# A two-block model step on one core: where the last token tile is turned, and when the last weight slabs are split

## Chip, cores, metric

One NeuronCore of one Trainium2 chip (trn2) runs the whole program. The metric is the time of one execution on the device in microseconds; lower is better. Everything is fp32 in memory.

## The reference

512 tokens of width 1024 go through a first block (three mixers, an MLP) and then through a second block of two layers, which the change is about. In short (`layer_norm`, `rms_norm` and the attentions are as their names say, and `swiglu(h, w_in, w_out)` is `(silu(gate) * up) @ w_out`):

```
for i in range(2):
    h = layer_norm(a * h + 0.5 * swiglu(h, ffa_w_in[i], ffa_w_out[i]), ...)
    proj = h @ mix_w_in[i]      # 1536 q,k,v columns, 512 z, 16 gates, then attention's
    # causal conv of 4, silu, l2 norm of q and k per head (64), gated delta rule, * silu(z)
    # stick-breaking attention, latent attention with rope
    mix = concat(o_gdn, o_sb, o_mla) @ mix_w_o[i]
    h = layer_norm(a * h + mix, ...)
    h = layer_norm(a * h + 0.5 * swiglu(h, ffb_w_in[i], ffb_w_out[i]), ...)
    h = h + sigmoid(h @ ple_w_gate[i]) * (p[i] @ ple_w_proj[i])
```

The feed-forward has 2816 inner columns. The result is `h`, 512 x 1024.

## The kernel before

**Operands.** Each projection is computed from operands split in two fp32r parts: `hi` is the rounded value, `lo` the rest. `mm3` (L243) makes three matmuls of one product: hi x hi, hi x lo, lo x hi. Weights come in slabs of 2048 fp32 a partition through a ring of three slots. SyncE loads a slab into `K.raw[z]`, ScalarE rounds it into `K.hi[z]`, VectorE subtracts into `K.lo[z]`; slab `j` uses slot `j % 3`. `ahead` (L442 for VectorE, L459 for ScalarE) is called as an engine walks over the slabs in program order, and splits up to one slab ahead of the one that TensorE is at. ScalarE's rounding waits until TensorE has used the slab that was in that slot (`w used`), and SyncE's load until that slab was split. `K.fences` (`stop`) hold the splitting back where the ring's memory is lent to another stage.

**Order.** Each engine's program is a list written by hand, stage by stage (`tensor_program`, `vector_program` and so on), and each engine works strictly in that order. Engines wait for each other by named points (`K.at`). PSUM banks are taken in rotation (`take`).

**Two shapes of projection.** `pe_fm` keeps a weight block stationary and streams all 512 tokens, so it needs all four token tiles of 128. `pe_tm` keeps a token tile stationary and streams up to 512 weight columns; a slab then holds 4 row blocks of 128.

**Closings.** The MLP, each feed-forward and each mixer output end with `pe_by_tile`: the last 512 of 1024 columns, whose two slabs are both taken at the start, tile by tile, 24 matmuls each. When a tile is complete, VectorE adds it to `hX` and applies the norm (`dve_ln`, or `dve_final` after the MLP). TensorE then transposes it (8 transposes, `pe_tiles`), and ScalarE and VectorE split the transposed tile into `hL` (`act_tiles`, `dve_tiles`), the operand of the next projection. `tiles_after` says that tile i-1 is transposed behind tile i, and tile 3 right behind tile 2 at the end. `pe_ple` closes layer 0 in the same way, without a norm. The walk `tm_walk` of ScalarE and VectorE calls `ahead` for a group of slabs and then handles its four tiles, so the second slab of a closing is split by VectorE behind the four tiles of the first 512 columns.

**Mixer input** (`pe_mx_in`, L2524). 12 blocks of 128 columns by `pe_fm`. Behind block f, `job(f - 1)` sums the squares of a q or k block on TensorE or transposes a v block. Then come the 16 gate columns by `pe_tm`, with 16-column matmuls on four tiles; then eight fp32 matmuls spread the reciprocal norms over the partitions (`mx rn`); then the 512 `z` columns. VectorE scales q and k by the spread norms (`dve_mx_scale`), computes the gates, and the delta rule begins.

**Attention** lends itself the ring's `hi` and `lo` memory (`lender`). The `raw` slots keep loading, but nothing is split until the stage is over (fence `ring back 4`). Behind it `act_split` and `dve_split` split the 8 blocks of `catT`, and only then the first slab of the mixer output.

## Time and profile before

| | us |
|---|---|
| runs, median of 3 (lowest, highest) | 4786.41 (4783.46, 4788.29) |
| profiled execution, whole time | 4790.0 |
| its span, first to last instruction | 4788.2 |
| TensorE busy (share of the span) | 4233.6 (88%) |
| VectorE, ScalarE, GpSimd busy | 2180.8, 1340.5, 156.6 |
| mean granted TensorE clock | 0.914 |

A row of the profile names the engine (PE is TensorE, PEld its weight loads, DVE VectorE, ACT ScalarE, POOL GpSimd, SP SyncE), the line of the kernel, the operation, output<-input and the shapes. Since helpers record all operations, L232 is every matmul, L239 every transpose, L286 every `tensor_tensor`, L297 every `scalar_tensor_tensor` and L336 every activation. `ring` is the lent or raw part of the weights' memory, `r` a rounded operand (`hi`, `lo`, `hL`), and `arena` the rest. A matmul `128*128 128x512` has 128 rows by 128 stationary columns and streams 512. Clock 1.00 is 2.4 GHz and 0.50 is 1.2 GHz.

### The profile page before, as it was taken

To read this page: it belongs to the slowest core of one execution; us is meant where nothing else is said; L and a number is where in the kernel's file an instruction comes from. 1 tells how busy PE (TensorE), PEld (TensorE's weight loads), DVE (VectorE), ACT (ScalarE), POOL (GpSimd) and SP (SyncE) were. 2 spreads that over 40 slices of the span, in tenths; PEclk is the share of its full clock that TensorE was granted. 3 is DMA by queue.
4 is the path that set the end of the run, shared out by engine and by line. 5 is a ranking of instruction groups with operands and counts; after the bars stand their busy time and mean duration, and the time that the engine had idled before them with its cause. 6 is when DMAs were issued, how large, how long until landed. Compare 5 with 4: busy or idle time off the path is not lost.

```text
span 4788.2 us, 69852 instructions
## 1 busy us (share of the span) xinstructions
PE 4233.6 (88%) x30212; PEld 3338.8 (70%) x30212; DVE 2180.8 (46%) x2940; ACT 1340.5 (28%) x1886; POOL 156.6 (3%) x194
## 2 busy tenths in 40 slices
PE   6987878878677999999987989998999987989998
PEld 3855768856455787788666667887788666567886
DVE  2135467753744444433636344334333636444334
ACT  3133233312122232322221342222222321342222
POOL 0000012120000000000001000000000001000000
PEclk8878979989889999999978989999999978999999
DMA  5101000033123323233200113232333200112331
GB/s 191 45 1 44 9 2 3 3 110 105 53 71 109 117 96 105 80 93 93 71 28 16 40 39 89 85 106 86 95 94 91 63 19 15 40 53 80 97 100 54
DMA packets 319059, 322.10 MB, mean 67 GB/s; under 512 B 10032, under 2 KB 243552, under 8 KB 317984
## 3 DMA queue, kind: packets, MB, share of 16 engines
q1 hardware_dynamic: 312144, 287.53, 19.5%
q0 software_dynamic: 6608, 30.11, 1.7%
q8 instruction: 238, 3.90, 0.3%
q14 instruction: 69, 0.57, 0.0%
...
## 4 chain that ended last, share of the span: by engine, by line
PE 77%; DVE 13%; issue 4%; ACT 4%; DMA 1%; POOL 0%; DVEq 0%; ACTq 0%; POOLq 0%
PE psum L232 76%; DVE ring L286 3%; DVE arena L297 3%; DVE ring L317 2%; DVE arena L286 2%; PE psum L239 1%; ACT arena L336 1%; ACT ring L336 1%; ACT r L336 1%; DVE r L286 1%; DVE arena L293 1%; DMA ring<-in_rw_g 0%; DVE arena L317 0%; DVE arena L291 0%; DVE ring L301 0%
## 5 line engine op out<-in xcount | busy, mean ns | idle before, releaser
L232 PE MATMUL psum<-r 128*128 128x512 f32 (+3 forms) x12912 | 3024.5, 396 | 157.0 <-DVE r L286 141.3
L232 PEld LDWEIGHTS psum<-r 128*128 128x128 f32 (+1 forms) x12912 | 2429.3, 195 | 748.6 <-DVE r L286 90.7
L286 DVE TENSOR_TENSOR r<-ring,r 128x2048 fp32r<-128x2048 f32 (+2 forms) x269 | 580.2, 2157 | 411.6 <-ACT r L336 400.6
L336 ACT ACTIVATE arena<-psum 128x512 f32<-128x512 f32 (+4 forms) x456 | 249.2, 547 | 1306.9 <-PE psum L232 1211.5
L336 ACT ACTIVATE r<-ring 128x2048 fp32r<-128x2048 f32 (+2 forms) x269 | 484.3, 1800 | 417.7 <-PE psum L232 341.1
L232 PE MATMUL psum<-arena 64*64 64x64 f32 (+14 forms) x2384 | 403.9, 337 | 48.7 <-DVE arena L286 17.8
L232 PE MATMUL psum<-ring 64*64 64x64 f32 (+4 forms) x8608 | 352.3, 236 | 84.2 <-ACT ring L336 34.8
L232 PEld LDWEIGHTS psum<-arena 128*128 128x128 f32 (+6 forms) x2384 | 265.2, 187 | 177.4 <-issue 131.7
L232 PEld LDWEIGHTS psum<-ring 64*64 64x64 f32 (+3 forms) x8608 | 290.6, 145 | 125.6 <-issue 47.5
L286 DVE TENSOR_TENSOR arena<-arena,psum 128x512 f32<-128x512 f32 (+2 forms) x192 | 114.9, 598 | 577.2 <-PE psum L232 570.2
L232 PE MATMUL psum<-ring,arena 64*64 64x64 f32 (+6 forms) x2464 | 265.4, 292 | 100.0 <-DVE ring L286 34.5
L297 DVE SCALAR_TENSOR_TENSOR arena<-arena 128x512 f32<-128x512 f32 (+4 forms) x316 | 266.7, 844 | 118.5 <-ACT arena L336 107.4
L232 PEld LDWEIGHTS psum<-ring,arena 64*64 64x64 f32 (+4 forms) x2464 | 148.8, 156 | 185.7 <-issue 136.9
L336 ACT ACTIVATE ring<-psum 128x512 f32<-128x512 f32 (+5 forms) x276 | 148.7, 539 | 457.6 <-PE psum L232 342.6
L336 ACT ACTIVATE r<-arena 128x512 fp32r<-128x512 f32 (+1 forms) x176 | 109.4, 622 | 530.4 <-DVE arena L286 528.4
L232 PE MATMUL psum<-arena,ring 64*64 64x64 f32 (+6 forms) x3072 | 203.7, 257 | 31.5 <-DVE ring L286 21.6
L286 DVE TENSOR_TENSOR arena<-arena 128x512 f32<-128x512 f32 (+7 forms) x273 | 171.1, 628 | 127.3 <-ACT arena L336 117.0
L286 DVE TENSOR_TENSOR arena<-psum,arena 128x512 f32<-128x512 f32 (+4 forms) x112 | 71.2, 636 | 343.9 <-PE psum L232 267.5
L232 PEld LDWEIGHTS psum<-arena,ring 64*64 64x64 f32 (+4 forms) x3072 | 166.7, 162 | 61.8 <-DVE ring L286 28.9
L286 DVE TENSOR_TENSOR r<-arena,r 128x512 fp32r<-128x512 f32 (+1 forms) x176 | 119.7, 680 | 157.4 <-ACT r L336 154.4
L336 ACT ACTIVATE arena<-arena 128x512 f32<-128x512 f32 (+10 forms) x181 | 78.1, 432 | 373.0 <-DVE arena L293 205.6
L239 PE MATMUL psum<-arena 128*128 128x128 f32 (+2 forms) x612 | 95.0, 307 | 98.7 <-DVE arena L291 48.0
...
## 6 DMA issues: line engine op xcount, KB each, us to landing
...
```

Of the source, the lines that this page charges most:

```text
L232: ins = self.raw.matmul(o, l, r, start=start, stop=stop, skip_group_check=True)
L239: ins = self.raw.transpose(o, i, self.K.C["ident"])
L286: self.done(self.raw and self.raw.tensor_tensor(o, a, b, f), keys)
L293: self.done(self.raw and self.raw.tensor_scalar(o, a, s1, s2, f0, f1), keys)
L297: self.done(self.raw and self.raw.scalar_tensor_tensor(out=o, in0=a, scalar=s, in1=b, op0=f0, op1=f1), keys)
L317: self.done(self.raw and self.raw.copy_predicated(o, m, d), keys)
L336: self.done(self.raw and self.raw.activation(o, i, f, scale=scale, bias=bias), keys)
```

## The change

- **Tiles.** `pe_tiles` transposes only tile i-1. Tile 3 is transposed inside the next projection. At a feed-forward's first slab and at the mixer input's first two blocks, `pe_halves` runs both blocks on tokens 0 to 255, then transposes tile 3 (`pe_tile`), then runs both on tokens 256 to 511. At the gated embedding, `pe_tm` waits by tile and transposes tile 3 ahead of its last tile. ScalarE and VectorE keep their order: they split tile 3 as the last step of the closing stage.
- **Slabs.** `tm_walk(both=True)` calls `ahead_of` once more before the four tiles of the first 512 columns in a closing stage.
- **Gate columns.** The 16 gate columns' weights become stationary with 512 tokens streamed, ahead of `job(11)`. ScalarE copies the 16 x 512 result, and four small matmuls turn it. The matmuls for the norms (`to_all`) move into `z`'s first slab, before its last tile, in the four banks that `z` does not hold.
- **Attention.** Each slot's `hi` and `lo` lie side by side; attention is lent those of slots 0 and 1 only, and the slab that follows it is put into slot 2 (`add_slab`, `next_slot`) and may be split before attention. `m.sq` and `m.st` move to scratch. Waits on `j - NSLOT` become waits on the last slab in the same slot.
- **`pT`** is loaded before the norm's rows on GpSimd's queue, without waiting for the end of the feed-forward.

```diff
+    def add_slab(self, pieces, size, split):
+        z = self.next_slot
+        self.slabs.append((pieces, size, split))
+        self.slot.append(z)
+        self.same_slot.append(self.last_in.get(z))
+        self.last_in[z], self.next_slot = len(self.slabs) - 1, (z + 1) % NSLOT
...
-            z, (_, size, split) = j % NSLOT, K.slabs[j]
+            z, (_, size, split) = K.slot[j], K.slabs[j]
-                if j >= NSLOT:
-                    a.wait_ge(*K.at("w used", j - NSLOT))
+                if K.same_slot[j] is not None:
+                    a.wait_ge(*K.at("w used", K.same_slot[j]))
...
+                if within and (done, k0, i) == (0, 0, len(tiles) - 1):
+                    within()
+                    if by_tile:
+                        t.wait_ge(*K.at(by_tile, "lo", i, q // 4))
...
-def tm_walk(E, ncols, kt, tiles, step=512):
+def tm_walk(E, ncols, kt, tiles, step=512, both=False):
+        if both and done == 0:
+            E.ahead_of()
...
+def pe_tile(t, K, st, x, ready):
+    t.wait_ge(*K.at(*ready, x))
+    for half in range(2):
+        o = t.take(st, "tr", x, half)
+        for q in range(4):
+            f = 4 * half + q
+            t.tr(o[:, 128 * q:128 * q + 128], K.m.hX[:, x, 128 * f:128 * f + 128],
+                 *([(st, "tr", x, half)] if q == 3 else []))
-    for x in tiles_after(i):
-        t.wait_ge(*K.at(*ready(x)))
-        for half in range(2):
-            o = t.take(st, "tr", x, half)
-            for q in range(4):
-                f = 4 * half + q
-                t.tr(o[:, 128 * q:128 * q + 128], K.m.hX[:, x, 128 * f:128 * f + 128],
-                     *([(st, "tr", x, half)] if q == 3 else []))
+    if i:
+        pe_tile(t, K, st, i - 1, ready)
+def pe_halves(t, K, wh, wl, blocks, st, ready):
+    for half in range(2):
+        c = slice(256 * half, 256 * half + 256)
+        for o, js, keys in blocks:
+            for k in range(8):
+                t.wait_ge(*K.at(st, "lo", 2 * half + 1, k // 4))
+                t.mm3(o[:, c], wh[:, k, js], wl[:, k, js], K.m.hL[:, 0, k, c], K.m.hL[:, 1, k, c],
+                      half == 0 and k == 0, half == 1 and k == 7, *(keys if half == 1 and k == 7 else []))
+        if half == 0:
+            pe_tile(t, K, st, 3, ready)
...
-                 *[(st, "lo", 4 * half + q) for q in range(4)])
+                 (st, "lo", x, half))
...
-def lender(K, first=SLOT * NSLOT):
+def lender(K, first=SLOT * NSLOT, end=RING):
-        assert used[0] <= RING, used[0]
+        assert used[0] <= end, used[0]
...
-    K.hi = [parts[:, SLOT * z:SLOT * z + SLOT] for z in range(NSLOT)]
-    K.lo = [parts[:, SLOT * (NSLOT + z):SLOT * (NSLOT + z) + SLOT] for z in range(NSLOT)]
+    K.hi = [parts[:, 2 * SLOT * z:2 * SLOT * z + SLOT] for z in range(NSLOT)]
+    K.lo = [parts[:, 2 * SLOT * z + SLOT:2 * SLOT * z + 2 * SLOT] for z in range(NSLOT)]
...
-    lend = lender(K)
+    lend = lender(K, end=RING - 2 * SLOT)
...
-    m.st = lend(128)
-    m.sq = lend(512)
+    m.sq, m.st = m.tmp[:, 0:512], m.tmp[:, 512:640]
+    m.pop = A.operand(2, 512)
+    m.sgp = view(al(2048), [512, 4], [1, 512])
+    A.top = base + 10240
-    m.pop = A.operand(2, 512)
-    K.base = base
-    m.sgp = view(al(2048), [512, 4], [1, 512])
...
             wh, wl = view(wh, [256, 8], [1, 256]), view(wl, [256, 8], [1, 256])
+            if part == 0 and f == 0:
+                blocks = [(t.take("ff1", l, j, 0, 0, u), slice(128 * u, 128 * u + 128),
+                           [("ff1", l, j, 0, 0, u)] + ([("w used", i)] if u else [])) for u in range(2)]
+                pe_halves(t, K, wh, wl, blocks, ready, source)
+                continue
             for u in range(2):
                 for k in range(8):
-                    t.wait_ge(*K.at(ready, "lo", k))
                     t.mm3(o, wh[:, k, js], wl[:, k, js], m.hL[:, 0, k, :], m.hL[:, 1, k, :], k == 0, k == 7,
     pe_by_tile(t, K, ("ff2", l, j, 2), Wo, 128 * FF_PARTS[2][0], 512, 512, FF_PARTS[2][1], m.hop, ("ff h", l, j, 2), 512,
-               lambda i: pe_tiles(t, K, st, i, lambda x: ("ln x", l, j, x)))
+               lambda i: pe_tiles(t, K, st, i, ("ln x", l, j)))
...
-    pe_fm(t, K, ("mx u", l), K.I["mix_w_in_2"][l], 0, 1536, 8, m.hL, lambda f: SEGS[0:1], ready=("hT", l, 0),
-          among=others, after=lambda f, g: job(f - 1))
+    W = K.I["mix_w_in_2"][l]
+    i, wh, wl = t.chunk(W, 0, 8, 0, 256)
+    blocks = [(t.take(("mx u", l), f, 0, among=others), slice(128 * f, 128 * f + 128),
+               [(("mx u", l), f, 0)] + ([("w used", i)] if f else [])) for f in range(2)]
+    pe_halves(t, K, wh, wl, blocks, ("hT", l, 0), ("ln x", l, 0))
+    job(0)
+    pe_fm(t, K, ("mx u", l), W, 0, 1536, 8, m.hL, lambda f: SEGS[0:1], among=others, after=lambda f, g: job(f - 1), start=256)
+    i, wh, wl = t.chunk(W, 0, 8, 2048, 16)
+    o = t.take("mx ab", l, among=others)
+    for k in range(8):
+        t.mm3(o[0:16, :], wh[:, k, :], wl[:, k, :], m.hL[:, 0, k, :], m.hL[:, 1, k, :], k == 0, k == 7,
+              *([("mx ab", l), ("w used", i)] if k == 7 else []))
-    pe_tm(t, K, ("mx ab", l), K.I["mix_w_in_2"][l], 2048, 16, 8, m.hL, W512)
-    for f in range(8):
-        o = t.take("mx rn", l, f)
-        t.wait_ge(*K.at("mx rn", l))
-        t.mm(o, m.hb[0:16, 128 * f:128 * f + 128], m.rn[0:16], True, True, ("mx rn b", l, f))
-    pe_tm(t, K, ("mx z", l), K.I["mix_w_in_2"][l], 1536, 512, 8, m.hL, W512)
+    def to_all():
+        z = [K.bank_of[("mx z", l), 0, i][0] for i in range(4)]
+        for f in range(8):
+            o = t.take("mx rn", l, f, among=tuple(b for b in BANKS if b not in z))
+            t.wait_ge(*K.at("mx rn", l))
+            t.mm(o, m.hb[0:16, 128 * f:128 * f + 128], m.rn[0:16], True, True, ("mx rn b", l, f))
+    o = t.take("mx ab T", l)
+    t.wait_ge(*K.at("mx ab sb", l))
+    for i in range(4):
+        t.mm(o[:, 16 * i:16 * i + 16], m.abT[0:16, 128 * i:128 * i + 128], C["ident"][0:16, 0:16], True, True,
+             *([("mx ab T", l)] if i == 3 else []))
+    pe_tm(t, K, ("mx z", l), W, 1536, 512, 8, m.hL, W512, within=to_all)
...
+    E.ahead()
+    a.wait_ge(*K.at("mx ab", l))
+    a.copy(m.abT[0:16], K.bank("mx ab", l)[0:16, :], ("mx ab sb", l))
+    K.free(a, "mx ab", l)
-    for _ in tm_walk(E, 16, 8, 4):
-        pass
...
+    E.ahead()
-    for c, i, _ in tm_walk(E, 16, 8, 4):
-        v.wait_ge(*K.at(("mx ab", l), c, i))
-        v.copy(m.gab[:, i, :], K.bank(("mx ab", l), c, i)[:, 0:16], ("mx gab", l))
-        K.free(v, ("mx ab", l), c, i)
+    v.wait_ge(*K.at("mx ab T", l))
+    v.copy(view(m.gab, [1, 64]), K.bank("mx ab T", l)[:, 0:64], ("mx gab", l))
+    K.free(v, "mx ab T", l)
...
     dve_split(v, K, ("cat", l), m.catT, m.hL, 8)
-    for c, i, _ in tm_walk(E, 1024, 8, 4):
+    for c, i, _ in tm_walk(E, 1024, 8, 4, both=True):
         x = m.hX[:, i, c:c + 512]
...
-    g.wait_ge(*K.at(("ff2", l, 2, 2), 512, 3))
-        pe_tm(t, K, ("ple g", l, hf), K.I["ple_w_gate_2"][l], 512 * hf, 512, 8, m.hL, W512, ready=("hT", l, "p"))
+        pe_tm(t, K, ("ple g", l, hf), K.I["ple_w_gate_2"][l], 512 * hf, 512, 8, m.hL, W512, by_tile=("hT", l, "p"),
+              within=None if hf else (lambda: pe_tile(t, K, ("hT", l, "p"), 3, ("ln x", l, 2))))
-                   lambda i: pe_tiles(t, K, ("hT", 0, 2), i, lambda x: ("ple x", 0, 1, x)) if (l, hf) == (0, 1) else None)
+                   lambda i: pe_tiles(t, K, ("hT", 0, 2), i, ("ple x", 0, 1)) if (l, hf) == (0, 1) else None)
...
         E.meet(f"attention {l}, ring lent")
+        if K.counting:
+            K.next_slot = NSLOT - 1
         pe_attention(E, K, l)
         E.meet(f"ring back 4 {l}")
-        K.fences[E.slab] = f"ring back 4 {l}"
+        K.fences[E.slab + 1] = f"ring back 4 {l}"
         pe_mix_out(E, K, l)
-        pe_ff(E, K, l, 2, "ffb_w_in_2", "ffb_w_out_2", ("hT", l, 1), ("hT", l, "p"))
+        pe_ff(E, K, l, 2, "ffb_w_in_2", "ffb_w_out_2", ("hT", l, 1), ("ln x", l, 1), ("hT", l, "p"))
         pe_ple(E, K, l)
...
         E.wait_ge(*K.at("ln x", l, 1, 3))
+        pool_ple(E, K, l)
         pool_ln(E, K, l, 2)
-        pool_ple(E, K, l)
         E.wait_ge(*K.at("ln x", l, 2, 3))
```

## Rows read from the trace of the kernel before

**Rows 1.** Page: busy time by engine; chain that ended last, by engine.
```profile
PE 4233.6 (88%) x30212; PEld 3338.8 (70%) x30212; DVE 2180.8 (46%) x2940; ACT 1340.5 (28%) x1886; POOL 156.6 (3%) x194
...
PE 77%; DVE 13%; issue 4%; ACT 4%; DMA 1%; POOL 0%; DVEq 0%; ACTq 0%; POOLq 0%
```

**Rows 2.** Waits of TensorE: total us, times, longest.
```profile
PE psum L232 <- DVE r L286: 141.3, 28, 17.9
...
PE psum L239 <- DVE arena L297: 27.6, 7, 4.0
```

**Rows 3.** Chain of waits, closing of layer 0's second feed-forward: start, us, what.
```profile
3271.15 0.87 PE psum L239 x8
3272.02 5.62 PE psum L232 x24
...
3284.16 0.70 DVE arena L297
...
3289.03 0.70 DVE r L286
...
3291.46 3.75 PE psum L232 x8
```

**Rows 4.** Groups by form, 549 to 557.6 us (busy us, mean ns).
```profile
L232 PE MATMUL psum<-r 128*128 128x256 f32 x24 | 3.1, 285 | 0.0
```

**Rows 5.** Timeline of the same closing: start, us, engine, what, [idle before].
```profile
3253.42 1.91 ACT L336 ACTIVATE r<-ring 128x2048 fp32r<-128x2048 f32 x1 [9.32 <-PE psum L232]
...
3254.70 4.67 DVE L286 TENSOR_TENSOR r<-ring,r 128x2048 fp32r<-128x2048 f32 x2
```

**Rows 6.** Timeline of TensorE, first slabs of the first and last closing.
```profile
1907.11 13.02 PE L232 MATMUL psum<-r 128*128 128x512 f32 x48 [3.76 <-DVE r L286]
...
4683.81 14.06 PE L232 MATMUL psum<-r 128*128 128x512 f32 x48 [3.75 <-DVE r L286]
```

**Rows 7.** Stretches: us, busy us per engine, then clock (PEclk), DMA share, GB/s.
```profile
2294.10:2308.30 14.20, 14.20 (x50) 11.19 (x51) 6.75 (x8) 0.20 (x1) 0.00 (x0) 0.78 0.47 148
...
2413.00:2433.60 20.60, 20.60 (x98) 20.60 (x97) 5.91 (x5) 7.71 (x7) 0.00 (x0) 0.50 0.17 52
2433.60:2447.60 14.00, 14.00 (x18) 5.19 (x17) 7.09 (x9) 0.00 (x0) 0.00 (x0) 0.50 0.23 75
...
549.00:557.60 8.60, 8.60 (x51) 7.46 (x50) 4.87 (x5) 2.92 (x5) 0.00 (x0) 1.00 0.00 1
...
3303.00:3340.00 37.00, 37.00 (x161) 29.76 (x160) 11.14 (x11) 8.38 (x9) 0.00 (x0) 1.00 0.32 85
```

**Rows 8.** Timeline, next projection behind the MLP and at layer 0's mixer input.
```profile
1940.22 81.15 PE L232 MATMUL psum<-r 128*128 128x512 f32 x337 [1.10 <-DVE r L286]
...
2328.65 12.49 PE L232 MATMUL psum<-r 128*128 128x512 f32 x48
```

**Rows 9.** Timeline of VectorE at that mixer input.
```profile
2329.46 0.92 DVE L321 MEMSET arena<- 128x1032 f32 x1 [0.16 <-issue]
...
2336.72 2.33 DVE L297 SCALAR_TENSOR_TENSOR arena<-arena 128x512 f32<-128x512 f32 x3
...
2339.75 0.69 DVE L286 TENSOR_TENSOR arena<-arena 128x512 f32<-128x512 f32 x1 [0.70 <-ACT arena L336]
```

**Rows 10.** Timeline at layer 0's gate columns.
```profile
2412.55 0.86 PE L239 MATMUL psum<-arena 128*128 128x128 f32 x4 [4.86 <-ACT arena L336]
...
2416.08 3.34 DVE L309 RECIPROCAL arena<-arena 16x512 f32<-16x512 f32 x1 [3.53 <-ACT arena L336]
```

**Rows 11.** Groups by form, 96 stationary columns.
```profile
L232 PE MATMUL psum<-r 128*96 128x512 f32 x96 | 22.7, 395 | 0.0
```

**Rows 12.** Timeline between attention and mixer output, layer 0.
```profile
2832.75 6.26 DVE L286 TENSOR_TENSOR r<-arena,r 128x512 fp32r<-128x512 f32 x8 [2.96 <-ACT r L336]
...
2841.64 20.59 PE L232 MATMUL psum<-r 128*128 128x512 f32 x78 [10.70 <-DVE r L286]
```

**Rows 13.** Timeline of VectorE before attention.
```profile
2695.33 0.69 DVE L286 TENSOR_TENSOR arena<-psum,arena 32x512 f32<-32x512 f32 x1 [17.87 <-PE psum L232]
```

More of the change, by code:

```diff
@@ L113, in __init__ @@
         self.signals, self.points, self.meets, self.slabs, self.fences, self.late = {}, {}, {}, [], {}, {}
+        self.slot, self.same_slot, self.last_in, self.next_slot = [], [], {}, 0
         self.counting = True
@@ L268, in weights @@
         if K.counting:
-            K.slabs.append((pieces, size, split))
-        z = i % NSLOT
+            K.add_slab(pieces, size, split)
+        z = K.slot[i]
         if split:
@@ L373, in load, with pe_fm @@
         K.points[("in", *key)] = (K.load_sem[z], K.loads[z])
-def pe_fm(t, K, st, W, c0, ncols, kt, xs, segs, ready=None, among=BANKS, after=None):
-    for done in range(0, ncols, 256):
+def pe_fm(t, K, st, W, c0, ncols, kt, xs, segs, ready=None, among=BANKS, after=None, start=0):
+    for done in range(start, ncols, 256):
         n = min(256, ncols - done)
@@ L397, in pe_fm, with pe_tm @@
                     after((done + m) // 128, g)
-def pe_tm(t, K, st, W, c0, ncols, kt, xs, tiles, r0=0, ready=None, step=512, among=BANKS):
+def pe_tm(t, K, st, W, c0, ncols, kt, xs, tiles, r0=0, ready=None, step=512, among=BANKS, by_tile=None, within=None):
     for done in range(0, ncols, step):
@@ L467, in ahead_of @@
             j = self.n_split
-            z, (_, size, split) = j % NSLOT, K.slabs[j]
+            z, (_, size, split) = K.slot[j], K.slabs[j]
             if split:
                 a.wait_ge(*K.at("w in", j))
-                if j >= NSLOT:
-                    a.wait_ge(*K.at("w used", j - NSLOT))
+                if K.same_slot[j] is not None:
+                    a.wait_ge(*K.at("w used", K.same_slot[j]))
                 a.copy(K.hi[z][:, 0:size], K.raw[z][:, 0:size], ("w hi", j))
@@ L480, in sync_program @@
     for j, (pieces, size, split) in enumerate(K.slabs):
-        z = j % NSLOT
+        z, b = K.slot[j], K.same_slot[j]
         if j in K.late:
             e.after(K.late[j])
-        if j >= NSLOT:
-            if K.slabs[j - NSLOT][2]:
-                e.wait_ge(*K.at("w hi", j - NSLOT))
-                e.wait_ge(*K.at("w lo", j - NSLOT))
+        if b is not None:
+            if K.slabs[b][2]:
+                e.wait_ge(*K.at("w hi", b))
+                e.wait_ge(*K.at("w lo", b))
             else:
-                e.wait_ge(*K.at("w used", j - NSLOT))
+                e.wait_ge(*K.at("w used", b))
         for fn, src in pieces:
@@ L871, in memory @@
     m.cv = view(al(1024), [512, 2], [1, 512])
-    m.rn = al(512)
+    m.rn, m.abT = al(512), al(512)
     m.hb = view(m.ktok, [1, 1024])
@@ L2288, in pe_mlp @@
     pe_by_tile(t, K, ("mlp2", 3), K.I["w_mlp2"], 3072, 512, 512, 8, m.hop1, ("mlp h", 3), 512,
[L2289 removed]
+               lambda i: pe_tiles(t, K, ("hT", -1, 2), i, ("fin x",)))
 def act_mlp(E, K):
@@ L2306, in act_mlp @@
             a.copy(m.hop1[:, 0, f, :], m.tmp1[:, 1024 + 512 * (f % 2):1536 + 512 * (f % 2)], (("mlp h", part), "hi", f))
-        for c, i, _ in tm_walk(E, 1024, 8, 4):
+        for c, i, _ in tm_walk(E, 1024, 8, 4, both=part == 3):
             if part == 3 and c:
@@ L2322, in dve_mlp @@
             v.tt(m.hop1[:, 1, f, :], o2, m.hop1[:, 0, f, :], SUB, (("mlp h", part), "lo", f))
-        for c, i, _ in tm_walk(E, 1024, 8, 4):
+        for c, i, _ in tm_walk(E, 1024, 8, 4, both=part == 3):
             o = m.tmp1[:, 512 * (i % 2):512 * (i % 2) + 512]
@@ L2430, with pe_ff @@
 FF_PARTS = ((0, 8), (8, 6), (14, 8))
-def pe_ff(E, K, l, j, wi, wo, ready, st):
+def pe_ff(E, K, l, j, wi, wo, ready, source, st):
     t, m = TensorLine(E, "ff"), K.m
@@ L2475, in act_ff @@
             a.copy(m.hop[:, 0, f, :], m.tmpf[:, 1024 + 512 * z:1536 + 512 * z], (("ff h", l, j, part), "hi", f))
-        for c, i, _ in tm_walk(E, 1024, nt, 4):
+        for c, i, _ in tm_walk(E, 1024, nt, 4, both=part == 2):
             if part == 0:
@@ L2503, in dve_ff @@
             v.tt(m.hop[:, 1, f, :], o2, m.hop[:, 0, f, :], SUB, (("ff h", l, j, part), "lo", f))
-        for c, i, _ in tm_walk(E, 1024, nt, 4):
+        for c, i, _ in tm_walk(E, 1024, nt, 4, both=part == 2):
             x = m.hX[:, i, c:c + 512]
@@ L3347, in act_mix_out @@
     act_split(a, K, ("cat", l), K.m.catT, K.m.hL, 8)
-    for c, i, _ in tm_walk(E, 1024, 8, 4):
+    for c, i, _ in tm_walk(E, 1024, 8, 4, both=True):
         if c:
@@ L3356, in dve_mix_out @@
     dve_split(v, K, ("cat", l), m.catT, m.hL, 8)
-    for c, i, _ in tm_walk(E, 1024, 8, 4):
+    for c, i, _ in tm_walk(E, 1024, 8, 4, both=True):
         x = m.hX[:, i, c:c + 512]
@@ L3526, in vector_program @@
         E.meet(f"attention {l}, ring lent")
+        E.ahead_of()
         dve_attention(E, K, l)
@@ L3578, in scalar_program @@
         E.meet(f"attention {l}, ring lent")
+        E.ahead_of()
         act_attention(E, K, l)
```

5 lines of the change are left out of this document (2 added, 3 removed).

## The prediction

> **What bounds the kernel now.** I read the page first: TensorE is busy 88% of the span and 77% of the chain that ended last, VectorE holds 13% of that chain, ScalarE 4% and DMA 1% [rows 1]. The reader is to see that TensorE sets the time and that what can be won lies in its idle stretches, which VectorE ends most often. The list of TensorE's waits names the two kinds that the change aims at: 28 waits for a VectorE write of an `r` tile (141.3 us) and 7 waits of 3.98 us for the layer norm [rows 2]. Then I read the timeline where one projection closes and the next begins, and last the granted clock by stretches.
>
> Unit prices: in an undisturbed closing, 24 matmuls of 512 columns take 5.62 us and 8 transposes 0.87 us in the chain [rows 3]. That is 0.234 us a matmul and 11.24 us for the 48 that use one full slab. At 256 columns 24 of them take 3.1 us at clock 1.00, 0.129 each [rows 4].
>
> **A. Both last slabs split together.** Seven projections close by tiles: the MLP, four feed-forwards, two mixer outputs. Each needs two slabs at its first tile, and the second one's `lo` is made on VectorE only after its two steps on the last tile of the columns before. TensorE stands 3.75 to 3.79 us; 7 times, 26.3 us. The 48 matmuls behind the gap are slow: 13.02, 14.26, 12.99, 14.07, 13.94, 12.98 and 14.06 us against 11.24 (the first and the last are shown [rows 6]), together 16.6 us. The clock of the second one is 0.78 [rows 7], so it runs partly at 1.2 GHz instead of 2.4, behind the idle time. After the change the slot of that slab is free when TensorE leaves the first slab of the earlier columns, 11.24 us before the gap's place. ScalarE's rounding (1.91) and VectorE's subtraction (2.3) need 4.2 [rows 5], so 7 us of cover is left. VectorE's first tile queues behind that split for about 1.5 us, and nobody waits for it, since tiles come 2.8 us apart. Gain 42.9; ends 26.3 (the slow clock stays) and 43.
>
> **B. The last tile turned inside the next projection.** From the last matmul of a closing to the next projection's first, the path is VectorE's norm (about 4.8 us from 3284.16), 0.87 of transposes and three 0.70 steps of splitting [rows 3]. The eight places cost 7.3, 7.35, 7.6, 7.5, 4.7, 7.5, 7.6 and 7.5 us (MLP, feed-forward, mixer output, feed-forward, gated embedding of layer 0, and the last three kinds again in layer 1), 57.0 in all [rows 3, 8]. After: 0.87 for tile 2, then a half projection (48 half-width matmuls, 6.2 us) that outlasts the 4.8 us of the norm, then 0.87 for tile 3. Then comes a wait for its first half: ScalarE 0.64, VectorE 0.70 and hand-overs, less the 0.44 that the second half's transposes cover, 1.1. Then the other half. The half width costs 96 x 0.129 - 48 x 0.234 = 1.15 us.
> - Four feed-forward starts: 2 x 0.87 + 1.1 + 1.15 = 4.0 each, 16. The second slab's split now queues behind tile 3 on both engines and is ready about 5.1 us after its transposes, while TensorE needs it after 7.3: no wait.
> - Two gated embeddings (full width, tile 3 turned after three tiles): 2 x 0.87 + 1.1, and there the second slab comes 1.2 late, since only 12 matmuls (2.8 us) stand between: 4.0 each, 8.
> - Two mixer inputs: 4.0, plus a new wait. Behind tile 3 VectorE has the clearing of `ubg` (0.92) and the split (2.29) before it convolves block 0 (0.5 + 2.33), then wait for ScalarE's SiLU (0.70) and square it (0.69) [rows 9]. That ends 11.0 us after the transposes, and both blocks end at 7.3: 3.7 us at the first sum of squares. 7.7 each, 15.4.
>
> Sum 39.4, gain 17.6. The clock cost here too: at the feed-forward after the MLP 337 matmuls took 81.15 instead of 79.0, and at the mixer input 48 took 12.49 instead of 11.24 [rows 8]; over the eight places some 16.6 us. The new stalls are shorter but not gone, so I count half, 8. Gain 25.6. Ends: nothing (no clock back and 2.2 us more queueing at each place) and 34.2.
>
> By the Trainium skill, page "TensorE: Matmul & The Clock Gate", section "Back-to-back issue gap", matmuls of 256 and 512 columns cost 262 and 518 cycles, so halving the width would cost next to nothing and the sum would gain about 6 us more. The trace disagrees: 0.129 against half of 0.234. The page "Perfetto Trace Analysis", section "Matmuls", says that larger matmuls are more efficient. That rule speaks against this edit, and the trace agrees, with 1.15 us a place.
>
> **C. Gate columns and norms.** In layer 0 from the last block (2407.1) to the end of `z` (2471.3) lie 64.2 us: a 4.86 wait for ScalarE's SiLU, 96 matmuls of 16 columns in 20.6, eight fp32 products of 512 columns in 14.0, `z` in 24; both middle stretches ran at clock 0.50 [rows 7, 10]. In layer 1 it is 65.8. After: 24 matmuls of 512 columns with 16 columns stationary (as 96 columns stationary, 22.7 us for 96 [rows 11]) take 5.65 and cover the wait for the SiLU. The last turns take 0.9, to 2413.3. Then `z`'s first slab is late: ScalarE rounds it after the SiLU (to 2414.4) and VectorE subtracts to 2416.7. Copying the gate rows and the four small products fit in that. `z` takes 22.5. The reciprocal of the norms (3.34 [rows 10]), now behind that split and ScalarE's root with its table load, ends near 2422.7, and TensorE asks for it at 2425.1. The eight products then cost 0.86 each at full clock (half of 14.0): 6.9. VectorE's scaling of 0.69 a block keeps pace, so four banks do. End 2446.1, plus 1.7 for a clock that falls behind the 3.4 us stall: 40.7. Gain 23.5, and 25.1 in layer 1: 48.6. Ends: 23 (clock at half throughout: 5.6 more for the gate columns, 7.1 for the products, in both layers) and 52.
>
> **D. Attention lends two slots.** Between attention and the mixer output TensorE stands 10.70 us: ScalarE and VectorE first split the eight blocks of `catT` (6.26 on VectorE), then the first slab [rows 12]. With the first slab split in the idle time before attention (VectorE stands 17.87 us there [rows 13]), the first matmul needs only block 0, at 2833.5: 8.1 earlier, less 0.3 because the first tile is paced by VectorE's 0.78 a block. VectorE is through with `catT` at 2839.0 and with the second slab 2.3 later; TensorE needs that at 2845. Gain 7.8 a layer, 15.6. The first 78 matmuls took 20.59 instead of 18.3 [rows 12]. I leave these 2.3 us as they are, since the clock may be low from attention's thin work; they are the upper end. Ends 10 and 20. The earlier load of `pT`, the moved scratch and the slot order count nothing: the loads are hidden by 5 us landings on a queue that is mostly idle; without that cover a late load would cost its 4 to 5 us.
>
> **Sum.** 42.9 + 25.6 + 48.6 + 15.6 = 132.7. The profiled execution took 4790.0 (span 4788.2 and 1.8 around it), so 4657; the median of the runs, 4786.4, lies 3.6 lower, so 4654. I forecast 4655. All good ends give 149, all bad ones 59.
>
> **Rivals.**
> 1. The clock does not come back. If the falls follow from changes in activity and not from these gaps, A keeps 26.3, B 17.6, C 23, D 15.6: 83, so 4704. For it: the gate columns ran at 0.50 although TensorE was busy all through [rows 7]. Against: the 37 us from 3303 have clock 1.00 with no gap in them [rows 7]. Chance 0.14.
> 2. The in-order queues take the place of the norm. ScalarE and VectorE now stand at tile 3 until its transposes come, so splits and first activations slip; with 5 us more at each of the eight places 40 us go: 4694. For it: the mixer input, where I already find 3.7. Against: VectorE is busy 46% of the span [rows 1]. Chance 0.17.
> 3. Slower: half clock that holds. The gate columns show TensorE fully busy and at 0.50 for 34.6 us [rows 7]. If half-width matmuls with a stall between them hold it so at all eight places, each loses 17.3 us, 138 in all, against 132.7 - 8 gained: 4786 + 13, 4800. It decides from about 31 us a place. Against: half-width matmuls ran at 1.00 from 549 on [rows 4, 7]. Chance 0.05.
> 4. The edits don't do what they say (the slab still comes last, the rows for the norms late): within 0.2%, chance 0.03.
>
> The page "TensorE: Matmul & The Clock Gate", section "HAM oscillation — how this bites in real kernels", says that idle gaps between bursts throttle the array each time. By that rule all the clock of A and B returns and the sum would be 8 us larger. The rows behind the gaps agree with it; the fully busy gate columns at 0.50 it does not explain by idle time alone.
>
> **How the numbers follow.** Main case 0.61, by itself 4635 to 4680. With rivals 1 and 2 the range is 4632 to 4706. What a measurement of this kernel can tell from no change is 0.2%, 9.6 us. Faster: 0.61 + 0.14 + 0.17 = 0.92; same 0.03; slower 0.05.
>
> **What would show it.** A is right if no 3.75 us gap stands before the 48 matmuls of a closing and they take 11.2 to 11.5 us. B is right if the time from the last full-width matmul of a closing to the end of the next slab's work falls from 18.6 to about 15.2, with one wait near 1.1 us; at the mixer input a wait near 3.7 us stands before the first sum. C: the stage from the last block to the end of `z` takes about 41 us and its clock is 1.00 for the most part; if it reads 0.50, rival 1 gains. D: 2 to 3 us instead of 10.70. A clock below 1.00 for tens of us behind the half-width matmuls would show rival 3 and make the prediction wrong.

## The result, and the profile after

The changed kernel takes 4665.2 us (median of four runs, 4662.8 to 4673.4), the kernel before 4784.9 (4783.2 to 4788.3): 0.9752 of the time, 95% interval 0.9735 to 0.9769. The forecast was 4655, in a range of 4632 to 4706. The profiled execution took 4664.5 (span 4662.7), 125.5 us less than that of before; the forecast said 132.7. By the medians the gain is 119.7.

In the rows of this kernel and of the experiments L241 is every matmul, L248 every transpose, L295 every `tensor_tensor`, L306 every `scalar_tensor_tensor` and L345 every activation. The list of TensorE's waits shows what went (total us, times, longest): the `r` waits of 141.3 us [rows 2] are 106.7, and the seven waits for the norm (27.6 us) are gone from the list's first ten.

```profile
PE psum L241 <- DVE r L295: 106.7, 26, 17.9
PE psum L241 <- DVE ring L295: 66.0, 30, 9.4
PE psum L241 <- ACT ring L345: 48.4, 27, 5.4
```

**The places of the change**, TensorE's timeline of after (start, length, what, [idle before <- who ended it]). First the closing behind layer 0's second feed-forward and the gated embedding, against [rows 3, 6]:

```profile
3194.66 18.20 PE L241 MATMUL psum<-r 128*128 128x512 f32 x77
...
3213.49 5.87 PE L241 MATMUL psum<-r 128*128 128x512 f32 x24
...
3226.47 8.65 PE L241 MATMUL psum<-r 128*128 128x512 f32 x36
3234.95 1.04 PE L248 MATMUL psum<-arena 128*128 128x128 f32 x8
3236.97 3.06 PE L241 MATMUL psum<-r 128*128 128x512 f32 x12 [0.98 <-DVE r L295]
3241.06 5.16 PE L241 MATMUL psum<-r 128*128 128x512 f32 x21 [1.03 <-DVE r L295]
```

The 3.75 us gap has gone, tile 3's transposes stand within the projection, and two short waits remain: 0.98 for its split (forecast 1.1) and 1.03 for the second slab (forecast 1.2). Next the place behind the MLP, where the forecast saw no further wait:

```profile
1923.45 5.86 PE L241 MATMUL psum<-r 128*128 128x256 f32 x48
1929.15 1.03 PE L248 MATMUL psum<-arena 128*128 128x128 f32 x8
1931.16 17.11 PE L241 MATMUL psum<-r 128*128 128x256 f32 x96 [0.98 <-DVE r L295]
1952.74 42.56 PE L241 MATMUL psum<-r 128*128 128x512 f32 x172 [4.48 <-DVE r L295]
```

The half-width start is there (the 96 are 48 of half and 48 of full width), and a new wait of 4.48 us ahead of the third slab. Layer 0's mixer input, gates and `z`, against [rows 7, 8, 10]:

```profile
2313.79 5.87 PE L241 MATMUL psum<-r 128*128 128x256 f32 x48 [0.98 <-DVE r L295]
2324.09 1.89 PE L241 MATMUL psum<-arena 128*16 128x512 f32 x2 [4.43 <-DVE arena L295]
2325.91 7.51 PE L241 MATMUL psum<-r 128*128 128x512 f32 x24
...
2392.98 5.77 PE L241 MATMUL psum<-r 128*16 128x512 f32 x24
2398.59 0.60 PE L248 MATMUL psum<-arena 128*128 128x128 f32 x4
2402.81 1.88 PE L241 MATMUL psum<-arena 16*128 16x16 f32 x8 [3.63 <-DVE arena L300]
2404.63 10.21 PE L241 MATMUL psum<-r 128*128 128x512 f32 x36
2414.77 10.54 PE L241 MATMUL psum<-arena 16*128 16x512 f32 x16
2425.25 15.75 PE L241 MATMUL psum<-r 128*128 128x512 f32 x60
```

The gate columns cost 5.77 us (forecast 5.65). But `z`'s first 36 matmuls take 10.21 instead of 8.4, the norm products 10.54 instead of 6.9, and the last 60 15.75 instead of 14.0. The windows of the same stretches (granted clock in the third column from the end) say why, and that TensorE was busy all the time:

```profile
2402.80:2414.70 11.90, 11.89 (x44) 9.65 (x44) 5.76 (x3) 3.91 (x4) 0.00 (x0) 0.78 0.55 178
2414.80:2425.20 10.40, 10.40 (x17) 3.83 (x16) 4.81 (x7) 0.00 (x0) 0.00 (x0) 0.67 0.00 0
2425.30:2440.80 15.50, 15.50 (x61) 12.46 (x61) 1.72 (x7) 6.56 (x10) 0.00 (x0) 0.90 0.00 0
```

At the mixer output the first matmul waits 2.65 us instead of 10.70 [rows 12]:

```profile
2801.54 36.51 PE L241 MATMUL psum<-r 128*128 128x512 f32 x144 [2.65 <-DVE r L295]
```

**Where the time went, by stages.** The profiled executions are cut at instructions that all kernels share, on VectorE unless said: "fin" is the last tile's reciprocal behind the MLP; "first" and "close" are the first statistics of a norm and its fifth (the closing's tile 0); "set" clears `ubg`; "z end" is the first small gate product on TensorE. The columns e1 to e12 are the experiments of the next section. Us from one mark to the next (five rows of layer 1 that repeat those of layer 0 within 1 us are left out):

```
to                  before  after   e1     e2     e3     e4     e10    e5     e6     e7     e8     e9     e11    e12
fin                 1936.2 1925.9 1925.7 1919.0 1928.4 1926.3 1922.5 1927.5 1928.5 1925.3 1925.2 1924.3 1922.9 1928.8
ffa0 first           346.5  348.2  347.3  347.3  348.1  348.1  348.1  348.8  341.2  348.1  348.1  348.2  341.3  341.2
ffa0 close            20.8   12.7   20.4   12.7   12.7   12.7   12.7   12.7   12.7   12.7   12.7   12.7   12.7   12.7
mx0 set               26.0   28.0   28.0   26.0   28.0   28.0   28.0   28.0   28.0   28.0   27.9   28.0   28.0   28.0
z0 end               141.9  126.1  125.9  124.8  143.6  126.1  126.1  125.0  126.3  122.3  122.1  115.4  111.6  114.8
mo0 first            387.4  379.8  383.2  380.4  386.8  383.9  395.1  383.7  383.9  383.4  381.1  387.1  380.6  387.8
mo0 close             19.6   12.6   19.6   12.6   12.6   12.6   12.6   12.6   12.6   12.6   12.6   12.6   12.6   12.6
ffb0 first           367.3  362.1  360.8  368.5  362.1  362.1  362.1  362.1  362.1  362.1  362.1  362.1  362.1  362.1
ffb0 close            20.6   12.7   20.8   12.7   12.7   12.7   12.7   12.7   12.7   12.7   12.7   12.7   12.7   12.7
ffa1 first           437.0  430.4  427.9  438.3  429.4  429.4  429.3  430.4  429.4  430.4  429.4  430.3  430.4  430.4
z1 end (from set)    143.3  125.6  124.4  124.8  142.2  124.3  126.5  124.1  124.4  122.6  119.4  113.5  110.4  114.8
mo1 first            392.4  381.3  385.0  383.5  382.2  386.2  390.8  382.8  382.9  381.0  381.7  379.9  386.3  388.8
end (from ffb1 cl.)   95.2   89.4   89.4   94.9   89.4   89.4   89.4   89.4   89.4   89.4   89.4   89.4   89.4   89.4
```

Two kinds of stage are to be told apart. Those of full matmuls repeat to 0.1 us from kernel to kernel where the code is the same ("ffa1 first", with the embedding in it, to 1.1). "fin" and "mo first" hold much thin work, and where the code up to them is the same ("fin": all but before and e1; "mo first": all but before, e10 and e12) they vary from 1919.0 to 1928.8 and from 379.8 to 387.1. So a median can't show an edit worth under 5 us; its stage can.

### The profile page after: what moved, and what is told of

It is laid out like the page before. It is cut to its first block, busy times and chain, and to the rows that moved or that the text cites. A ratio compares the mean times of both kernels' runs of the same rounds, so it can differ in the third digit from the quotient of the medians.

```text
span 4662.7 us, 70153 instructions
## 1 busy us (share of the span) xinstructions
PE 4166.8 (89%) x30372; PEld 3297.4 (71%) x30372; DVE 2180.1 (47%) x2934; ACT 1340.6 (29%) x1888; POOL 157.7 (3%) x194
## 4 chain that ended last, share of the span: by engine, by line
PE 69%; issue 12%; DVE 12%; ACT 4%; DMA 1%; POOL 0%; DVEq 0%; ACTq 0%; SPq 0%; POOLq 0%
PE psum L241 68%; DVE ring L295 2%; DVE arena L306 2%; DVE ring L326 2%; DVE arena L295 2%; PE psum L248 1%; ACT arena L345 1%; ACT r L345 1%; ACT ring L345 1%; DVE r L295 1%; DVE arena L302 1%; DMA ring<-in_w_ada 0%; DVE arena L300 0%; DMA ring<-in_rw_g 0%; DVE arena L326 0%
## 5 line engine op out<-in xcount | busy, mean ns | idle before, releaser
L241 PE MATMUL psum<-r 128*128 128x512 f32 (+3 forms) x13056 | 2977.3, 389 | 122.4 <-DVE r L295 106.7
L241 PEld LDWEIGHTS psum<-r 128*128 128x128 f32 x13056 | 2392.2, 191 | 701.8 <-DVE r L295 79.1
L295 DVE TENSOR_TENSOR r<-ring,r 128x2048 fp32r<-128x2048 f32 (+2 forms) x269 | 580.4, 2158 | 452.4 <-ACT r L345 442.5
L345 ACT ACTIVATE arena<-psum 128x512 f32<-128x512 f32 (+3 forms) x458 | 250.3, 546 | 1249.7 <-PE psum L241 1158.0
L345 ACT ACTIVATE r<-ring 128x2048 fp32r<-128x2048 f32 (+2 forms) x269 | 484.5, 1801 | 406.1 <-PE psum L241 330.2
L241 PE MATMUL psum<-arena 64*64 64x64 f32 (+15 forms) x2400 | 399.6, 334 | 62.9 <-DVE arena L295 26.6
L241 PE MATMUL psum<-ring 64*64 64x64 f32 (+4 forms) x8608 | 351.0, 235 | 84.7 <-ACT ring L345 34.3
L241 PEld LDWEIGHTS psum<-arena 128*128 128x128 f32 (+7 forms) x2400 | 264.8, 186 | 187.8 <-issue 125.3
L241 PEld LDWEIGHTS psum<-ring 64*64 64x64 f32 (+3 forms) x8608 | 289.2, 144 | 124.5 <-issue 46.2
L295 DVE TENSOR_TENSOR arena<-arena,psum 128x512 f32<-128x512 f32 (+2 forms) x192 | 114.8, 598 | 552.6 <-PE psum L241 545.6
L241 PE MATMUL psum<-ring,arena 64*64 64x64 f32 (+6 forms) x2464 | 258.4, 289 | 100.2 <-DVE ring L295 33.0
L306 DVE SCALAR_TENSOR_TENSOR arena<-arena 128x512 f32<-128x512 f32 (+4 forms) x316 | 266.7, 844 | 119.0 <-ACT arena L345 107.7
L345 ACT ACTIVATE ring<-psum 128x512 f32<-128x512 f32 (+5 forms) x276 | 148.7, 539 | 451.2 <-PE psum L241 374.2
L241 PEld LDWEIGHTS psum<-ring,arena 64*64 64x64 f32 (+4 forms) x2464 | 147.1, 156 | 181.9 <-issue 132.2
L345 ACT ACTIVATE r<-arena 128x512 fp32r<-128x512 f32 (+1 forms) x176 | 109.4, 622 | 518.8 <-DVE arena L295 516.8
L295 DVE TENSOR_TENSOR arena<-arena 128x512 f32<-128x512 f32 (+8 forms) x289 | 176.8, 613 | 127.9 <-ACT arena L345 117.0
L241 PE MATMUL psum<-arena,ring 64*64 64x64 f32 (+6 forms) x3072 | 201.7, 255 | 32.6 <-DVE ring L295 21.9
L241 PEld LDWEIGHTS psum<-arena,ring 64*64 64x64 f32 (+4 forms) x3072 | 166.4, 161 | 61.2 <-DVE ring L295 30.1
L295 DVE TENSOR_TENSOR arena<-psum,arena 128x512 f32<-128x512 f32 (+4 forms) x112 | 71.2, 636 | 292.6 <-PE psum L241 235.0
L295 DVE TENSOR_TENSOR r<-arena,r 128x512 fp32r<-128x512 f32 (+1 forms) x176 | 119.8, 681 | 157.3 <-ACT r L345 154.4
L345 ACT ACTIVATE arena<-arena 128x512 f32<-128x512 f32 (+10 forms) x181 | 78.1, 432 | 323.1 <-DVE arena L302 168.1
L326 DVE COPY_PREDICATED ring<-arena,psum 128x512 f32<-128x512 uint32 (+1 forms) x202 | 136.0, 679 | 37.5 <-PE psum L241 30.9
```

Of the source, the lines that this page charges most:

```text
L241: ins = self.raw.matmul(o, l, r, start=start, stop=stop, skip_group_check=True)
L295: self.done(self.raw and self.raw.tensor_tensor(o, a, b, f), keys)
L306: self.done(self.raw and self.raw.scalar_tensor_tensor(out=o, in0=a, scalar=s, in1=b, op0=f0, op1=f1), keys)
L326: self.done(self.raw and self.raw.copy_predicated(o, m, d), keys)
L345: self.done(self.raw and self.raw.activation(o, i, f, scale=scale, bias=bias), keys)
```

## The experiments

**Each part undone alone.** In e1 the three walks lose `both`. e2 turns tile 3 behind tile 2 and starts at full width:

```diff
 def pe_tiles(t, K, st, i, ready):
     if i:
         pe_tile(t, K, st, i - 1, ready)
+    if i == 3:
+        pe_tile(t, K, st, 3, ready)
```

e3 puts back the old `act_mx_in` and `dve_mx_in`, the 16-column matmuls, and the products ahead of `z`. e4 drops the two added calls `E.ahead_of()` ahead of attention, and e10 the shifted fence too:

```diff
-            K.fences[E.slab + 1] = f"ring back 4 {l}"
+            K.fences[E.slab] = f"ring back 4 {l}"
```

e1: 

> Part A undone alone: the second of the two last slabs is split at the first tile of the last columns again, seven closings. Theory (gap and slow clock belong together): between the traces of before and after, the aligned points give 5.0 to 6.8 us a closing, 42 in all, so this kernel takes 4665 + 42 = 4707 us; a gap near 3.8 us stands before each closing and the 48 matmuls behind it take 13 to 14 us. Rival (the clock recovered for other reasons): only the gaps of 3.75 us come back, 26 us, 4691, and the 48 matmuls stay at 11.2 to 11.5.

e2: 

> Part B undone alone: tile 3 is turned right behind tile 2 and every projection behind it starts at full width, once all of its input is split; the gated embedding too. Theory (the eight places gave 23 us by the aligned points: 6 to 8 each behind feed-forwards, 5 to 8 at the embedding, but -0.3 at the feed-forward behind the MLP and -2.3 and -1.3 at the two mixer inputs): 4665 + 23 = 4688, and the stage from layer 0's feed-forward to the end of block 11 of the mixer input gets about 2 us shorter than in the kernel after. Rival (what the aligned points show at these places is the clock's own coming and going, and only the shorter waits count): 4665 + 9 = 4674.

e3: 

> Part C undone alone: 96 matmuls of 16 moving columns for the gates, the eight norm products before z. Theory: the stage from the turn behind block 11 to the end of z goes back to 64 to 66 us in both layers, +33 us, 4698. Rival (the part is worth what was forecast and the rest was lost elsewhere by the change of phase): +48.6, 4714.

e4: 

> Part D undone in its effect: the two slots are still lent and loaded early, but ScalarE and VectorE split the first slab of the mixer output after the eight blocks of catT. Theory: the split in the idle time before attention is all of the gain, the gap of 10.7 us comes back in both layers, +16 us, 4681. Rival (part of the gain is the earlier load): less than +12 us, a gap under 8 us.

e10: 

> Part D undone for good: the fence stands before the mixer output's first slab again and no slab is split before attention, so it is loaded and split behind the eight blocks of catT. Theory (the place of the split is the gain; in e4 the ordinary look-ahead had already made it, so the explicit call changed nothing): the gap of 2.65 us becomes 10.7 in both layers, +16 us, 4681. Rival (e4's reading: the part is worth 3 us): 4668.

Measured: e1 4707.6 us, e2 4689.7, e3 4704.6, e4 4668.1, e10 4685.1 (0.9833, 0.9799, 0.9828, 0.9753 and 0.9789 of before, intervals of plus or minus 0.0015). Against 4665.2 the parts are worth 42.4, 24.5, 39.5 and, by e10, 19.9, 126 in all, where the whole change gives 119.7. The intervals are 7 us to either side, so each of these differences is known to some 10 us only, and the stages say more. e1's closing has the gap and the slow matmuls behind it again, where after has neither, as the first theory says (4707 expected):

```profile
2284.42 13.83 PE L241 MATMUL psum<-r 128*128 128x512 f32 x48 [3.75 <-DVE r L295]
```

e2's timeline at the mixer output has the wait for the norm and the transposes at half speed behind it; its stages say 6.4 and 6.3 us at the second feed-forwards, 7.9 over the first embedding and the feed-forward behind it, 5.5 at the last embedding, but -0.9 behind the MLP and -3.3 and -2.7 at the mixer inputs (both stages to "z end" added):

```profile
2845.36 1.97 PE L248 MATMUL psum<-arena 128*128 128x128 f32 x8 [3.98 <-DVE arena L306]
2847.98 4.25 PE L241 MATMUL psum<-r 128*128 128x512 f32 x10 [0.65 <-DVE r L295]
```

e3's stages give C 17.5 and 16.6, 34.1 in all, as its theory says (33); the median lies between theory and rival. e4's theory fell: its wait at the mixer output is 2.65 us as in after, since with the fence one slab later the ordinary look-ahead splits that slab anyway (VectorE's split stands at 2658.23, ahead of attention, as in after at 2654.23), and the added calls do nothing. e10 undoes what matters, and the old wait is back, in both layers:

```profile
2814.66 35.18 PE L241 MATMUL psum<-r 128*128 128x512 f32 x144 [10.70 <-DVE r L295]
```

**The price of half width (e5).**

```diff
-                for k in range(8):
-                    t.mm3(o, wh[:, k, js], wl[:, k, js], m.hL[:, 0, k, :], m.hL[:, 1, k, :], ...
+                for c in (slice(0, 256), slice(256, 512)):
+                    for k in range(8):
+                        t.mm3(o[:, c], wh[:, k, js], wl[:, k, js], m.hL[:, 0, k, c], m.hL[:, 1, k, c], ...
```

> The disputed unit price by itself: all 84 remaining feed-forward blocks run as 96 matmuls of 256 columns instead of 48 of 512, with nothing else changed. Theory (the trace after shows 48 of them in 5.70 us, 0.119 each, so the width costs 0.2 us a block): +10 to +20 us, 4675 to 4685. Rival (0.129 each, as the prediction read it: 1.15 us a block): +97 us, 4762.

4674.5 us by the median, 9 more than after, but hardly any of it in the changed stages: "ffb0 first", with 21 slabs halved, is 362.1 us in both, and all four feed-forwards together are 1.4 us longer for 84 slabs. Half width costs next to nothing, and the rival's 97 us are refuted. The 277 matmuls of the timeline stand 32.48 / 277 = 0.117 us apart, half of 0.234:

```profile
2867.78 32.48 PE L241 MATMUL psum<-r 128*128 128x256 f32 x277
```

**Three orders (e6, e7, e8).** e6 moves the rotary tables from block 0 to block 4 in both queues. e7 moves one call, e8 two:

```diff
-    job(0)
-    pe_fm(..., after=lambda f, g: job(f - 1), start=256)
+    pe_fm(..., after=lambda f, g: (f == 2 and job(0), job(f - 1)), start=256)
```

```diff
 def act_mx_in(E, K, l):
...
         K.free(a, ("mx u", l), f, 0)
+        if f == 11:
+            E.ahead()
         a.wait_ge(*K.at("mx conv", l, f))
...
-    E.ahead()
     a.wait_ge(*K.at("mx ab", l))
 def dve_mx_in(E, K, l):
...
-    E.ahead()
     v.wait_ge(*K.at("mx sums", l, 7))
...
     K.free(v, "mx sums", l)
+    E.ahead()
```

e6: 

> The rotary tables (about ten small VectorE steps and two sines on ScalarE) are made at block 4 of layer 0's first feed-forward instead of block 0. Theory (they stood in both queues ahead of the split of the third slab, which the half start needs 6 us sooner after tile 3's turn, and made the new 4.48 us wait): the wait goes, the clock behind it holds, -4.5 to -7 us, 4659 to 4661. Rival (the splits of tile 3 and of the slab are late by themselves): the wait stays above 3 us, no change.

e7: 

> At the mixer input the first sum of squares is issued behind block 2 instead of before it. Theory (TensorE waits 4.43 us there for block 0's square, which nobody needs before block 2's square): the wait goes in both layers, -8.9 us and up to 2 us of clock each, 4652 to 4656. Rival (the wait only moves: block 2's weights or the convolution of block 1 are late next): -2 us or less.

e8: 

> Gates: VectorE makes the sum for the norms before it splits z's first slab (it frees the bank that the turned gate rows take), and ScalarE rounds that slab before the last SiLU. Theory (the 3.63 us stall is this order, and the low clock of the norm products comes from the stall): the stall falls under 1 us and the sixteen passes of the norm products take 7 us instead of 10.5, so -3 - 3.5 - up to 2 for z, in both layers: -13 to -17 us, 4648 to 4652. Rival (the fp32 products on 16 rows lower the clock themselves): the stall goes but the products stay at 9 to 10.5 us, -6 us, 4659.

Measured: 4665.5, 4665.7 and 4654.8 us. By the medians e6 and e7 are worth nothing, by their stages 7.0 us (348.2 to 341.2) and 3.8 and 3.0; e11 below shows these gains in a median too. In e6 no wait stands behind the first 0.97, so the first theory holds:

```profile
1933.75 61.63 PE L241 MATMUL psum<-r 128*128 128x256 f32 x287 [0.97 <-DVE r L295]
```

e7 is between its two theories: of 4.43 us of waiting, 0.28 + 1.67 + 0.72 remain, because VectorE convolves and splits without a pause there:

```profile
2319.32 5.86 PE L241 MATMUL psum<-r 128*128 128x512 f32 x24 [0.28 <-DVE r L295]
2325.11 1.03 PE L241 MATMUL psum<-arena 128*16 128x512 f32 x2
2327.81 1.03 PE L241 MATMUL psum<-arena 128*16 128x512 f32 x2 [1.67 <-DVE arena L295]
...
2335.36 1.03 PE L241 MATMUL psum<-arena 128*16 128x512 f32 x2 [0.72 <-DVE arena L295]
```

e8 settles the cause of C's loss, timeline and windows of the same stretches:

```profile
2398.70 1.03 PE L241 MATMUL psum<-arena 16*128 16x16 f32 x8 [0.33 <-ACT arena L345]
2399.67 8.66 PE L241 MATMUL psum<-r 128*128 128x512 f32 x36
2408.26 11.65 PE L241 MATMUL psum<-arena 16*128 16x512 f32 x16
```

```profile
2399.70:2408.20 8.50, 8.50 (x37) 6.65 (x36) 5.77 (x3) 4.83 (x5) 0.00 (x0) 1.00 0.41 125
2408.30:2419.80 11.50, 11.50 (x17) 4.12 (x16) 4.82 (x7) 0.00 (x0) 0.00 (x0) 0.60 0.27 90
2419.90:2435.90 16.00, 16.00 (x61) 12.81 (x61) 1.72 (x7) 6.56 (x10) 0.00 (x0) 0.86 0.00 0
```

The stall is 0.33 instead of 3.63 us and `z` starts at full clock, but the norm products fall to 0.60 with TensorE busy before and during them. The rival was right: they lower the clock themselves. In layer 0 the 112 matmuls of `z` and products take as long as in after (8.66 + 11.65 + 16.29 = 36.6 us against 36.5), so without the stall the same clock is lost later, and what is gained is the stall and the faster gate products in front of it. In layer 1 they take 34.9 instead of 37.6. The stage gains 4.0 and 6.2.

**The products in rounded passes (e9).**

```diff
-            t.mm(o, m.hb[0:16, ...], m.rn[0:16], True, True, ("mx rn b", l, f))
+            t.mm(o, m.hb[0:16, ...], m.rr[0:16, 0], True, False)
+            t.mm(o, m.hb[0:16, ...], m.rr[0:16, 1], False, True, ("mx rn b", l, f))
```

`rr` holds the norms in two rounded parts, made by one copy on ScalarE and one subtraction on VectorE.

> The order of e8, and the eight norm products as two passes of rounded operands (the norms split in two by ScalarE and VectorE, the zeros and ones exact) instead of fp32 passes: again sixteen matmuls of 512 columns on 16 rows. Theory (fp32 passes on 16 rows lower the clock, 0.58 with TensorE busy all through in e8, and the rounded ones don't): sixteen at 0.234 would take 3.8 us, held up by VectorE's scaling to 5 to 6, and the 60 matmuls of z behind take 14.1 us instead of 16.3 and 16.8: about 8 us a layer less than e8, 4639. Rival (16 rows are what lowers it): 7 us for the products, z as slow as before: -3 a layer, 4649.

4649.1 us; its stages are 6.7 and 5.9 shorter than e8's. The rival's time (4649) and its mechanism came out, since passes on 16 rows lower the clock when rounded too, but more is gained than the 3 us a layer that it allowed. Products and `z` are 112 matmuls in 29.82 us, not 26.2, and the clock falls towards the end of the products, while TensorE is busy:

```profile
2398.90 29.82 PE L241 MATMUL psum<-r 128*128 128x512 f32 x112
```

```profile
2407.00:2409.00 2.00, 2.00 (x10) 1.34 (x9) 0.69 (x1) 0.00 (x0) 0.00 (x0) 1.00 0.66 145
2409.00:2412.00 3.00, 3.00 (x10) 2.01 (x9) 2.63 (x4) 0.00 (x0) 0.00 (x0) 0.65 0.65 253
2412.00:2415.00 3.00, 3.00 (x8) 1.93 (x7) 2.62 (x7) 0.15 (x1) 0.00 (x0) 0.50 0.00 0
2415.00:2418.00 3.00, 3.00 (x11) 2.40 (x10) 0.59 (x4) 2.92 (x5) 0.00 (x0) 0.71 0.00 0
```

The rounding pays in two ways of like size. Against full clock e9 loses 3.00 x (0.35 + 0.50 + 0.29) = 3.4 us here, e8 by its windows 11.50 x 0.40 + 16.00 x 0.14 = 6.8: the low clock lasts half as long. The other 3 us are the shorter passes.

**All of it (e11).** The edits of e6 to e9 in one.

> Rotary tables at block 4, first sum of squares behind block 2, gate order of e8, rounded norm products of e9, all in one. Theory (the stages add: -6.9 for the rotary tables, -3.8 and -3.0 for the sum, -4.0 and -6.2 for the order by the stages of e6, e7 and e8, and -16 for the products): 4665 - 40 = 4625. Rival (the clock gives back what the waits lose, since a stage with fewer waits is throttled elsewhere): 4640 or more.

4631.3 us (4627.0 to 4635.3), 0.9680 of before, interval 0.9667 to 0.9693: the best kernel here, 34 us under after. Its stages gain 6.9, 14.5 and 15.2, 36.6 in all, nearly the 40 expected; the rival (4640 or more) is refuted.

**The products spread (e12).** In e11's `pe_tm`, instead of all products ahead of `z`'s fourth tile:

```diff
+                    if between and k % 2 and 4 * k0 // kn + i >= len(tiles) - 1:
+                        next(between, None)
```

> As e11, but the eight norm products don't stand together: one (two passes on 16 rows) behind every six matmuls of z from its fourth tile on. Theory (the clock falls to 0.50 because some twenty passes on 16 rows stand in a row, among them the rounded ones, as the spacing of 0.43 instead of 0.23 us from the twelfth product on in e9 shows): between full matmuls it stays at 1.00, and the 112 matmuls of z and products take 26.3 to 26.8 us instead of 29.8 to 30.1, -3.5 a layer, 4624. Rival (the clock's fall there has another cause, or the products hold up z through their banks): 29 us or more, 4631 or more.

4652.1 us, 21 slower than e11. The mechanism was right and the price wrong; the rival's numbers came out, but neither of its reasons. The clock stays at 1.00, yet the 112 matmuls take 29.48:

```profile
2392.26 29.48 PE L241 MATMUL psum<-r 128*128 128x512 f32 x112
2425.36 4.44 PE L241 MATMUL psum<-arena 128*128 128x32 f32 x20 [3.62 <-ACT arena L345]
```

```profile
2402.00:2408.00 6.00, 6.00 (x23) 3.48 (x22) 1.86 (x3) 0.00 (x0) 0.00 (x0) 1.00 0.38 144
2408.00:2414.00 6.00, 6.00 (x23) 3.52 (x21) 1.57 (x3) 0.00 (x0) 0.00 (x0) 1.00 0.00 0
```

Single starts of that trace stand 0.33, 0.34, 0.32 and 0.34 us apart around each product and 0.234 elsewhere: 0.4 us a product, 3.2 a layer, about what the clock would have given. Besides, the last scaling now comes late, ScalarE's gate work behind it holds up its reading of `z`, and the small gate products wait 3.62 us and run at clock 0.50 (4.44 us). The stages to "z end" lose 3.2 and 4.4, those to "mo first" 7.2 and 2.5, and "fin", where the code is the same, 5.9.

## Why the prediction was right, and where its terms were off

- **A, forecast 42.9, measured 42.4.** Both halves of the term held: the closings ("close") went from between 19.6 and 20.8 us down to 12.7, gap and slow clock together, and the clock over them reads 1.00. In e1 the stages "first" of the feed-forwards are 0.9 to 2.5 us shorter than in after. At least part of that is the mark itself: in after VectorE's first statistics queue behind the earlier split (2271.15 to 2273.44, the mark at 2274.07), as the prediction allowed for with about 1.5 us. "first" and "close" together are 6.8, 6.8, 4.4 and 6.7 us shorter in after than in e1 at the four feed-forwards.
- **B, forecast 25.6, measured 24.5 (by e2's stages 19.2).** Right in the sum, wrong in its parts, and the sum is partly luck: errors of both signs cancel, and by the stages it was 6 us too high. The step "the half width costs 96 x 0.129 - 48 x 0.234 = 1.15 us" failed: 0.129 came from a group's busy time [rows 4] which counts the last matmul to its end, not to the next start; e5 shows 0.117 and next to no cost. There the Trainium skill was right and my reading wrong: by its page "TensorE: Matmul & The Clock Gate", section "Back-to-back issue gap", halving the width costs next to nothing. The prediction's remark that the trace agrees with a cost of small matmuls rests on the same misreading and falls with it. Feed-forwards returned more than forecast: this cost fell away, and with it the slow matmuls that e2 shows behind its wait (10 in 4.25 us). Against that stand two things. The step "the second slab's split ... no wait" held for the second slab, but the third was late behind the MLP: on both queues the rotary tables (10 us of small VectorE steps) stood ahead of it, 4.48 us and a slower clock, shown by e6. And the wait at the first sum of squares was 4.43 instead of 3.7 and took the clock with it, so that at the mixer inputs full width would have been 3 us better; with e7's order the two are even (150.3 against 150.8 us over both stages in layer 0).
- **C, forecast 48.6, measured 39.5 (34.1 by e3's stages).** In layer 0 the way from the last block (2392.63) to the end of `z` (2440.83) is 48.2 us instead of 40.7. The mis-sized term is the clock: "the eight products then cost 0.86 each at full clock", 6.9, measured 10.54, at 0.67. "1.7 for a clock that falls behind the stall" was 1.8 at `z`'s first part and 1.7 more at its last; and the small gate products, which I had put inside the stall, came behind it, 1.9. The stall itself was 3.63 (forecast 3.4) but for another reason: the turned gate rows take the bank of the sums, which VectorE freed only behind the split; with both orders changed e8 has 0.33. What I had listed for rival 1, a half clock with TensorE busy all through [rows 7], was the sign: there the clock may have fallen in the wait of 4.86 us ahead, but it stayed low through 34.6 us without idle time. For the norm products e8 shows that the narrow work itself does it; for the 16-column matmuls no run takes the wait away.
- **D, forecast 15.6, measured 19.9.** The waits fell by 8.05 each, 16.1, but the 144 matmuls behind them take 36.51 us in after and 35.18 and 35.96 in e10, so 14 are shown. The rest is within what the stages around attention vary.
- **The rivals.** 1 holds in one place, the norm products. 2 happened in three places (4.48 behind the MLP, 4.43 at both mixer inputs, where 3.7 was forecast), not in eight. 3 did not: the half-width matmuls run at full clock. 4 is refuted by e1 to e3 and e10.

By the profiled executions the sum was 7.2 us too high (132.7 against 125.5). The other 3 us of the miss come from the step to a median: the forecast lies 2 us under what the profile gave, but after's profiled execution came out 0.6 below its median. That the parts add up to 126 by medians and not to 119.7 is within their uncertainty.
